# Chunk-state products of a hybrid SSD / gMLP step: from one fp32 product to three fp32r passes, with the bursts placed anew

## The reference

```
xc = (x * dt[..., None]).reshape(bsz, nc, SSD_CHUNK, h, p)
a_cum = jnp.cumsum(a_dt, axis=-1)
decay_states = jnp.exp(a_cum[..., -1:] - a_cum)
states = jnp.einsum('bcshn,bhcs,bcshp->bchpn', bh, decay_states, xc)
```

## Time and profile before

| | |
|---|---|
| median of three runs | 1425.21 us |
| profiled execution | 1425.4 us |
| its span (first to last instruction) | 1423.7 us |
| PE busy | 1406.9 us, 99% |
| DVE busy | 996.9 us, 70% |
| ACT busy | 463.8 us, 33% |
| POOL busy | 1022.5 us, 72% |
| PE's share of the chain that ended last | 97% |

### The profile page before, as it was taken

How to read it: one execution, slowest core, us unless ns; L and a number is a source line. 1 busy time by engine, 2 the same in 40 slices (tenths; PEclk the granted TensorE clock), 3 DMA queues, 4 the chain that set the end, 5 groups by cost and what they waited for, 6 DMA issues and landing times.

```text
span 1423.7 us, 26029 instructions
## 1 busy us (share of the span) xinstructions
PE 1406.9 (99%) x9631; PEld 1348.3 (95%) x9631; DVE 996.9 (70%) x1470; ACT 463.8 (33%) x1055; POOL 1022.5 (72%) x1421
## 2 busy tenths in 40 slices
PE   8999999999999999999999999999999999999997
PEld 5899998999999999999998999989999999999997
DVE  5837578665777679989978666966666876868234
ACT  4312133213756333001242233231266661310122
POOL 1778886586645589998859798747765556979772
PEclk9999999999999999999999999999999999999999
DMA  9121656123566565444332255631246665343222
GB/s 362 61 75 64 194 155 178 53 75 106 170 188 177 166 246 204 138 162 147 109 134 75 75 156 153 170 104 60 102 129 182 187 184 198 140 184 119 75 75 89
DMA packets 170667, 199.97 MB, mean 140 GB/s; under 512 B 55232, under 2 KB 137280, under 8 KB 169152
## 3 DMA queue, kind: packets, MB, share of 16 engines
q1 hardware_dynamic: 94000, 150.93, 31.9%
q10 hardware_dynamic: 76560, 47.54, 11.7%
HBM read 175.03 MB, written 23.40 MB: 139 GB/s over the span
## 4 chain that ended last, share of the span: by engine, by line
PE 97%; DVE 1%; DMA 1%; ACT 0%; SPq 0%; issue 0%; ACTq 0%; DVEq 0%
PE acc L645 79%; PE X L612 5%; PE acc L612 3%; PE X L876 2%; PE X L841 2%; PE X L861 1%; PE X L907 1%; DMA ada_pre<-in_wada 1%; PE X L887 1%; PE acc L763 0%; DVE h_pre L1507 0%; DVE xr L1982 0%; PE X L848 0%; PE X L823 0%; PE X L895 0%; DVE h_lo L1501 0%
## 5 line engine op out<-in xcount | busy, mean ns | idle before, releaser
L551 POOL CAST w_hi<-w_st 128x256 fp32r<-128x256 f32 x704 | 411.0, 598 | 379.0 <-PE acc L645 173.2
L555 POOL TENSOR_TENSOR w_lo<-w_st,w_hi 128x256 fp32r<-128x256 f32 x704 | 649.5, 932 | 0.0
L645 PE MATMUL acc<-h_hi,w_hi 128*128 128x320 f32 x1744 | 405.5, 314 | 0.8 <-ACT h_hi L1068 0.8
L645 PE MATMUL acc<-h_lo,w_hi 128*128 128x320 f32 x1744 | 397.8, 309 | 1.1 <-DVE h_lo L1501 1.1
L645 PE MATMUL acc<-h_hi,w_lo 128*128 128x320 f32 x1744 | 397.4, 309 | 0.0
L645 PEld LDWEIGHTS acc<-h_hi,w_hi 128*128 128x128 f32 x1744 | 289.6, 188 | 12.1 <-issue 7.8
L645 PEld LDWEIGHTS acc<-h_lo,w_hi 128*128 128x128 f32 x1744 | 291.4, 188 | 1.8 <-DVE h_lo L1501 1.7
L645 PEld LDWEIGHTS acc<-h_hi,w_lo 128*128 128x128 f32 x1744 | 291.5, 188 | 0.0
L1662 DVE SCALAR_TENSOR_TENSOR cv<-raw,convw_sb,cv 128x642 f32<-128x642 f32 x128 | 137.4, 1073 | 4.5
L1414 DVE SCALAR_TENSOR_TENSOR ada_acc<-ada_st,sc,ada_acc 128x512 f32<-128x512 f32 x112 | 106.8, 992 | 1.8
L1660 DVE TENSOR_SCALAR cv<-raw,convw_sb 128x642 f32<-128x642 f32 x32 | 26.7, 834 | 73.3 <-ACT raw L1204 73.2
(11 more groups left out here) (254 smaller groups left out, 2296.4 us busy)
## 6 DMA issues: line engine op xcount, KB each, us to landing
w_st<-in_wts SPq DMA_DIRECT2D x176, 512.0 KB, 3.5
cum_bc<-cum_dram ACTq DMA_DIRECT2D x80, 256.0 KB, 4.9
ada_st<-in_wada SPq DMA_DIRECT2D x33, 512.0 KB, 4.4
ex_bc<-ex_dram ACTq DMA_DIRECT2D x64, 128.0 KB, 3.0
ada_pre<-in_wada SPq DMA_DIRECT2D x15, 512.0 KB, 10.0
xs<-xs_dram SPq DMA_DIRECT2D x64, 80.0 KB, 3.4
mga_dram<-c_buf SPq DMA_DIRECT2D x16, 320.0 KB, 6.2
xf<-xf_dram SPq DMA_DIRECT2D x4, 1280.0 KB, 7.0
```

The source lines that it names most:

```text
L551: nc.gpsimd.tensor_copy(quarter(w_hi, slot, q), quarter(w_st, slot, q)).then_inc(s_pool, 1)
L555: nc.gpsimd.tensor_tensor(quarter(w_lo, slot, q), quarter(w_st, slot, q), f(quarter(w_hi, slot, q)), ALU.subtract).then_inc(w_split, 1)
L645: last = mm(a[:, hf, 0:n1], w[:, s, cols], x[:, k, hf * HALF:hf * HALF + n1], start=(k == 0 and n == 0), stop=(k == KC - 1 and n == 2))
```

## The change

The chunk states' product is now made like the projections, in three fp32r passes. ScalarE makes the upper parts `bt_hi` (from the PSUM bank, in place of the plain copy `bt`) and `xw_hi` (a new instruction, 128x512). VectorE makes the lower parts `xw_lo = xw - xw_hi` (128x512) and `bt_lo = X[2] - bt_hi` (128x128), in a new function `a_low`. PE waits for `low_ready` instead of `bt_ready` and `xw_ready`, and issues three matmuls instead of one.

The bursts get new places: burst 0 stays at (20, 7); bursts 1 to 3 are at tiles 22, 23 and 24, chunk 2; then two per tile at chunks 2 and 6 of tiles 25 to 31; the last three at tile 32, chunks 2, 5 and 8. Before, they were at tiles 20 to 24, then three per tile from tile 25. Unit 6's weights leave the convolution loop, `a_low(0)` to `a_low(3)` enter it behind i = 12 to 15, and the later ones stand in `order_dve` just behind the due time of the burst that made their transpose. The six scan steps move two tiles later. `xw_hi` and `bt_lo` lie in memory that `uz` blocks 4 and 5 use from tile 32 on, so ScalarE's evacuation of tile 32 now waits for the last product; `scan_tmp` lies where `xw` and the second `cum_bc` buffer are, so only that buffer's load waits for the scan.

```
-A_AT = [(20 + a, 2 + 5 * (a == 0)) for a in range(5)] + [(25 + a // 3, 2 + 3 * (a % 3)) for a in range(16)]
+A_AT = [(20, 7), (22, 2), (23, 2), (24, 2)] + [(25 + a // 2, 2 + 4 * (a % 2)) for a in range(14)] + [(32, k) for k in (2, 5, 8)]
...
-            13: (("a", 3),), 14: (("x", 4), ("a", 4)), 15: (("a", 5), ("x", 5), ("a", 6))}
+            13: (("a", 3),), 14: (("x", 4), ("a", 4)), 15: (("x", 5), ("a", 5))}
...
-    out += [(8 * p + k, "a", n) for n, (p, k) in enumerate(A_AT) if 7 <= n < NU]
+    for n, (p, k) in enumerate(A_AT[:NU]):
+        if n >= 4:
+            out += [(8 * p + k + 1.2, "low", n)]
+            if n + 2 < NU:
+                out += [(8 * p + k + 1.3, "a", n + 2)]
...
-    out += [(8 * 27 + 6 + 3 * c, "ln", c) for c in range(NCH)] + [(8 * (31 + i) + 1.5, "scan", i) for i in range(6)]
+    out += [(8 * 27 + 6 + 3 * c, "ln", c) for c in range(NCH)] + [(8 * (33 + i) + 1.5, "scan", i) for i in range(6)]
...
-                pe.wait_ge(bt_ready, n)
-                pe.wait_ge(xw_ready, n)
+                pe.wait_ge(low_ready, n)
...
-                mm(X[3][:, cols], bt[:, s, :], xw[:, s, :, :, :].rearrange("p d h w -> p (d h w)")[:, cols],
-                   start=True, stop=True).then_inc(s_mm, 1)
+                for i, (b, x) in enumerate(((bt_hi, xw_hi), (bt_lo, xw_hi), (bt_hi, xw_lo))):
+                    last = mm(X[3][:, cols], b[:, s, :], x[:, s, :, :, :].rearrange("p d h w -> p (d h w)")[:, cols],
+                              start=(i == 0), stop=(i == 2))
+                last.then_inc(s_mm, 1)
...
-                    A(bt[:, a % 2, :], X[2][:, 0:P], ACT.Copy).then_inc(bt_ready, 1)
+                    A(bt_hi[:, a % 2, :], X[2][:, 0:P], ACT.Copy)
+                    act.wait_ge(xw_ready, n + 1)
+                    A(xw_hi[:, a % 2, :, :, :].rearrange("p d h w -> p (d h w)"),
+                      xw[:, a % 2, :, :, :].rearrange("p d h w -> p (d h w)"), ACT.Copy).then_inc(up_ready, 1)
...
+                    if n == 8:
+                        act.wait_ge(s_mm, NU * (L + 1))
...
                if a >= 2:
-                    dve.wait_ge(s_mm, n - 1)
+                    dve.wait_ge(low_ready, n - 1)
...
+            def a_low(a):
+                n = NU * L + a
+                dve.wait_ge(up_ready, n + 1)
+                s = a % 2
+                flat = [w[:, s, :, :, :].rearrange("p d h w -> p (d h w)") for w in (xw_lo, xw, xw_hi)]
+                TT(flat[0], flat[1], f(flat[2]), ALU.subtract)
+                TT(bt_lo[:, s, :], X[2][:, 0:P], f(bt_hi[:, s, :]), ALU.subtract).then_inc(low_ready, 1)
...
+                if i >= 12:
+                    a_low(i - 12)
                 for what, n in READY_AT.get(i, ()):
```

More of the change, by code:

```diff
@@ L261, in build @@
     yab = place("yab", [P, 2, GC], r_t + 18432)
-    scan_tmp = place("scan_tmp", [P, DM], r_t + 4096)
     wsp_sb = place("wsp_sb", [P, 8, P], r_t + 8192)
@@ L274, in build @@
     xw = place("xw", [P, 2, 2, HPG, HD], r_c + 2 * TOK * 4)
-    bt = place("bt", [P, 2, P], r_c + 2 * TOK * 4 + 4096)
+    bt_hi = place("bt_hi", [P, 2, P], r_c + 2 * TOK * 4 + 4096, F32R)
+    xw_hi = place("xw_hi", [P, 2, 2, HPG, HD], r_uz + 10240, F32R)
+    bt_lo = place("bt_lo", [P, 2, P], r_uz + 14336, F32R)
+    scan_tmp = place("scan_tmp", [P, DM], r_c + 2 * TOK * 4)
     dtx = place("dtx", [P, 4, NCH, 32], r_uz)
@@ L291, in build @@
     r_ex = region(2 * GC * 4)
+    xw_lo = place("xw_lo", [P, 2, 2, HPG, HD], r_cum, F32R)
     ex_bc = [place(f"ex_bc{i}", [P, 2, GC], at) for i, at in enumerate((r_cum, r_ex))]
@@ L352, in build @@
     xs_in, xt_done, ln_ready = [sem("xs_in0"), sem("xs_in1")], sem("xt_done"), sem("ln_ready")
-    bt_mm, bt_ready, xw_ready, s_mm, s_out = sem("bt_mm"), sem("bt_ready"), sem("xw_ready"), sem("s_mm"), sem("s_out")
+    bt_mm, xw_ready, s_mm, s_out = sem("bt_mm"), sem("xw_ready"), sem("s_mm"), sem("s_out")
+    up_ready, low_ready = sem("up_ready"), sem("low_ready")
     scan_done, vvar, vroot = sem("scan_done"), sem("vvar"), sem("vroot")
@@ L1273, in _ @@
                         act.wait_ge(ex_stored, 32 * (L + 1))
+                        load_cum(0)
+                    if n == 14:
                         act.wait_ge(scan_done, L + 1)
-                        load_cum(0)
                         load_cum(1)
@@ L1793, in _ @@
                     a_unit(n)
+                elif what == "low":
+                    a_low(n)
                 elif what == "bn":
```

## The result

| | before | after |
|---|---|---|
| median | 1425.63 us (4 runs, 1425.17 to 1426.27) | 1445.69 us (4 runs, 1444.99 to 1446.26) |
| profiled execution, its span | 1425.4, 1423.7 us | 1446.11, 1443.5 us |
| DVE busy | 996.9 us | 1036.3 us |
| ACT busy | 463.8 us | 484.1 us |

The changed kernel takes 1.0140 times as long (95% interval 1.0127 to 1.0152), 20.1 us more. The forecast was 1447.

A forecast was written before the change was run, and what follows sets the result against it. PE, busy 99% of the span, was taken as the bound. Per layer -2.7 for products, +7.1 and +6.5 for waits make +10.9, over two layers +21.8 on 1425.4: 1447 us, range 1432 to 1456.

The forecast's parts named there:

- PE is the bound, and what it waits is lost: Whole kernel: PE is busy 99% of the span, so what it saves is saved and what it waits is lost.
- The products: PE's chunk-state products: three fp32r passes take 0.68 us instead of 0.86, or 0.36 instead of 0.43; 5.4 us saved over two layers.
- The moves of places cost nothing: Bursts at new places: chunks and transposes stay the same in number, so their moves alone cost PE nothing.
- `a_low` is 1.1 us: VectorE's lower parts for one unit: 0.82 + 0.28 = 1.1 us, with ends of 0.95 and 1.4 us.
- Waits in tiles 22 to 25: Bursts (22, 2) to (25, 2): late DVE makes PE wait 0.5, 2.3, 2.4 and 1.9 us, 7.1 us a layer.
- Waits from tile 25 on: Two bursts per tile: DVE's in-order, nearly full queue makes PE wait 6.5 us a layer, bounds 0 and about 12.
- my walk: The 16 bursts from tile 25, each DVE piece at its earlier duration: 1.4 us at (26, 6), 2.6 at (32, 5).
- DVE's total: DVE's work from (25, 2) to tile 33: 53.2 less 4.7 plus 17.6, 66 us against some 70 of PE's.
- A: Rival: DVE keeps up, the subtractions fit into gaps and PE gets its 5.4 us, 1420 us; 4 in 100.
- B: Rival: only the convolution stretch loses, two bursts per tile leave enough room from tile 25, 1434 us; 17 in 100.
- C: Rival: PE's clock falls in the waits, 3.5 us behind each of nine longer waits per layer, 1510 us; 3 in 100.
- The scan and tile 32's evacuation: From tile 32: scan steps hidden in tiles 33 to 38; evacuation about 1 us late, its accumulator next used 7 us on.

The follow-up runs named there:

- experiment 1: Changed kernel without lower parts: three passes of upper parts alone, PE waiting for ScalarE's copies, no VectorE subtraction; 1419.08 us, 0.9954 of the kernel before.
- experiment 2: Changed kernel's new places alone, with the fp32 product and plain copies of the kernel before; 1423.94 us, 0.9991 of the kernel before.
- Experiment 3: Changed kernel with lower parts of units 0 to 3 earlier in VectorE's order, ahead of the SiLU product; 1438.14 us, 1.0084 of the kernel before.
- experiment 5: Changed kernel with unit 18's lower part moved ahead of tile 31's gates and `yg_lo`; 1441.71 us, 1.0115 of the kernel before.
- experiment 6: Changed kernel with `yg_hi` and `yg_lo` of three blocks moved behind the neighbouring unit's parts; 1438.99 us, 1.0096 of the kernel before.
- experiment 7: Changed kernel with the three rearrangements of experiments 3, 5 and 6 together; 1427.76 us, 1.0014 of the kernel before.
- experiment 9: Changed kernel with ten units per layer in three passes, the rest one fp32 product, and lower and yg parts reordered; 1421.09 us, 0.9965 of the kernel before.

## Why the prediction was right

- **PE is the bound, and what it waits is lost.** Right. The changed kernel has 22.4 us of waits at its products where the one before had 1.4, and PE's busy time moved by 1 us.
- **The products.** 0.68 and 0.36 us were predicted; three starts 0.23 and 0.12 apart were found. The term was -5.4 us and measured -4.9 (experiments 1 and 2).
- **The moves of places cost nothing.** They gain 1.6 us (the interval reaches down to 0). Most of it is 0.6 us of small waits a layer, at the bursts (26, 5) and (29, 2), which I had called too little to count.
- **`a_low` is 1.1 us.** In the convolution stretch it is 0.88 + 0.28 less an overlap of 0.1 us, as taken. From tile 25 on the subtraction is mostly shorter, 0.68 us where GpSimd stands still (298.76 in layer 0), below the 0.75 that I gave as its least, so the mean is 0.767.
- **Waits in tiles 22 to 25.** Predicted ready times 197.5, 207.7, 217.6 and 227.3 us; the products start 0 to 0.6 us behind these. Predicted waits 0.5, 2.3, 2.4 and 1.9, sum 7.1 us a layer; measured 0.81, 2.17, 1.74 and 1.76, sum 6.5. Experiment 3 takes most of them away by moving the work and nothing else, so the mechanism (DVE's queue is late, and `a_low` makes it later) is shown.
- **Waits from tile 25 on.** Predicted 6.5 us a layer, measured 4.5 and 4.9. The term was mis-sized, chiefly at (26, 6) and (27, 2): 2.1 us together in the forecast, 0.37 at 240.4 and 0.11 at 244.6 in the trace. The prices of the pieces are not the reason at (26, 6). From the weights behind the `a_low` before it to the end of its own `bt_lo` DVE takes 6.0 us:

```profile
234.39 1.10 DVE L1655 TENSOR_TENSOR xw<-x_tok,ex 128x256 f32<-128x256 f32 x2
...
240.08 0.28 DVE L1666 TENSOR_TENSOR bt_lo<-X,bt_hi 128x128 fp32r<-128x128 f32 x1
```

At the prices of before the same pieces come to about the same, so my walk was wrong in what stands there or in DVE's lead over PE; which, stays open. DVE's total was too high as well, 66 us against 62.1. A scan step is two instructions, and I took off only the first, 4.7 us; the window before also holds the second:

```profile
L1712 DVE TENSOR_TENSOR states<-states,scan_tmp 128x1024 f32<-128x1024 f32 x2 | 2.5, 1262 | 0.1
```

The sixteen `a_low` took about 15 us instead of 17.6, and the gates a little more than before. (32, 5) was right (2.6 against 2.43), and so were the places (30, 6) and (31, 6). But I held DVE's `yglo` alone responsible. That fits (30, 6). At (31, 6) the row says ACT's `xw_hi`. At (32, 5) both engines are late, as experiments 5 to 7 show: with the lower part ahead on DVE 1.64 us of the wait stay, with `yg_hi` and `yg_lo` behind 1.70, and with both changes nothing. I had checked ACT's load, not where a wait of its own stands in its order.
- **Not foreseen.** Behind each of some 22 waits PE loses another 0.11 us until the products follow at their pace, about 2.4 us, and one fall of the clock costs 1.6. With 22.4 us of waits that is 26.4, against the 26.6 between experiment 1 and the changed kernel. In the total, 4.8 us of waits fewer than the 27.2 predicted are nearly made up by these 4.0. That 1447 came within 1.3 us is therefore luck in part: the mechanism holds, but two terms were off by 4 to 5 us each, in opposite directions.
- **The rivals.** A (DVE keeps up, 1420 us) fails: that is about the time of experiment 1, where DVE has no lower parts to make. B (only the convolution stretch) fails by the 4.5 to 4.9 us of later waits. C (the clock falls) happened once and is a term, not a case: what I priced at 3.5 us was 1.6, and of the 14 waits over 0.5 us 13 had no fall.
- **The scan and tile 32's evacuation.** From tile 33 to the end the traces run in parallel: tile 33 of layer 1 starts at 1004.74 us, before at 984.90, which is 19.8 later, and the span is 19.8 longer.

## What to carry to other kernels

An engine that is busy for 70% can still be the one that ends last: look where its queue is late, and price new work at those places, not over the span. Check an order for each engine that the new chain passes, ACT too: an instruction that waits for something else ahead of a copy can hold PE up as a full engine does. Where a cheaper form of an instruction needs preparation, use it only at places where the preparing engine has room; ten of twenty products a layer, with the new places and a better order, brought 4.4 us where all twenty lost 20.

## What the runs showed of the hardware

- After a wait on a semaphore the first fp32r matmul takes 0.10 to 0.11 us longer to the next one's start (0.34 against 0.23 us at 512 columns, 0.22 against 0.12 at 256), even where the wait is as short as 0.11 us (244.63 in the changed kernel).
- PE's clock fell to 0.50, its 1.2 GHz level, behind some waits and not behind others of the same length. In the changed kernel the wait of 2.43 us at (32, 5) had a fall in layer 0 and none in layer 1; with the doubled subtraction there were 8 falls, two of them behind waits of 1.94 us. The Trainium skill, page "TensorE: Matmul & The Clock Gate", section "HAM oscillation — how this bites in real kernels", describes it in a kernel that pauses for 3 to 5 us; here a fall followed pauses of 2 to 3 us at times, and the one at (32, 5) cost 1.6 us. Such a fall is nearly free where PE would wait at the next product anyway. In experiment 6 the wait of 2.18 us at (23, 2) had one in layer 0, and there the wait at (24, 2) was gone; in layer 1 it had none, and (24, 2) waited 1.75 us. Some executions also have the clock at 0.50 from about 39.5 to 43 us, in the opening, ahead of all that these kernels change (the profiles of experiments 2, 3 and 9; in that of experiment 7 from 38.8 to 45.7). The runs of experiment 2 lie in two groups, seven from 1423.7 to 1424.4 us and four from 1425.0 to 1425.7, and the profiled one, in the upper group, has this fall, so it is likely what sets single executions apart by 1.2 us or so.
- `xw_lo`, 128x512 with two SBUF inputs, takes 0.83 to 0.98 us beside a busy GpSimd (16 of the 40 in the changed kernel) and 0.67 to 0.69 where GpSimd stands still for all or nearly all of it (the other 24). The Trainium skill's rule on who interferes with whom (page "SBUF — State Buffer", section of that name), cited in the prediction, agrees; `bt_lo`, with one input from PSUM, took 0.28 or 0.29 us everywhere.
